# A split becomes an entry of the memory attention's walk, mixed rows are split one step sooner, and GpSimd's first small loads wait for the input's last tile

## The chip, the cores and the metric

One NeuronCore of a Trainium2 chip runs the whole program. The metric is the device time of one execution in microseconds. Three runs of the kernel before gave 2355.81, 2359.80 and 2361.21 us; the median is 2359.8 us.

## The reference, cut to what matters

Two transformer blocks over 512 tokens of width 1024, all in float32. The first block has a mixer (dilated window attention with 8 heads beside a retention with 4), a cross attention to a memory of 256 tokens, and a hierarchical mixture of 32 experts. The second has two layers of attention and a squared-ReLU MLP. The change touches the start of the mixer, its output projection, and the cross attention to the memory:

```python
def memory_cross_attention(h, mem_h, w_mq, w_mkv, q_norm_w, k_norm_w, w_mo):
    q = rms_norm(split_heads(h @ w_mq, MEM_HEADS, MEM_HEAD_DIM), q_norm_w) * (MEM_HEAD_DIM ** -0.5)
    mk, mv = jnp.split(mem_h @ w_mkv, 2, axis=-1)
    k = rms_norm(split_heads(mk, MEM_HEADS, MEM_HEAD_DIM), k_norm_w)
    v = split_heads(mv, MEM_HEADS, MEM_HEAD_DIM)
    s = jnp.einsum('bhsd,bhmd->bhsm', q, k, preferred_element_type=jnp.float32)
    p = jax.nn.softmax(s, axis=-1)
    o = jnp.einsum('bhsm,bhmd->bhsd', p.astype(v.dtype), v)
    return merge_heads(o) @ w_mo

x = x + parallel_mixer(rms_norm(x, norm_mix_w), w_in, ...)
x = x + memory_cross_attention(rms_norm(x, norm_mem_w), rms_norm(mem, norm_memkv_w), ...)
x = x + hierarchical_moe(rms_norm(x, norm_moe_w), ...)
```

There are 4 heads of width 256 here. The 512 queries are 4 token tiles of 128 rows, so there are 16 tiles of 128 queries x 256 keys.

## The kernel before, in words

**Projections.** Each float32 factor is split in two: a high part (rounded to the type fp32r that TensorE takes at full rate) and a low part (the factor less its high part). A product is three matmuls: high x high, high x low, low x high (`three`, L461; `products`, L455). Activations stand transposed in FH and FL. Weights come as units of 1 MB (a quarter-depth panel of 512 x 512 times two) into four raw buffers R; ScalarE writes the high part (`act_cut`, L441, 128 x 2048) and then VectorE the low part (`dve_cut`, L449). A third pair of split buffers serves some units of the memory stage. SyncE sends unit u only once the low part of unit u - 4 is done. A panel of 512 columns needs two units (its half 0 and half 1 of the depth), and `projecting` (L490) walks a list of steps (half, token tile), each of 12 matmuls of 128 x 512.

**Order of work.** Each engine has its own program order, written out by hand; engines wait for each other by semaphores only. Attention is walked (`walk`, L841): a list of entries is passed with a lag for each kind of work. In step s an engine does the scores of entry s, the transposes of the weights of entry s - 2 ("turn"), their products with the values of s - 3 ("apply"), and for an entry whose pair completes a half of a token tile "finish" of s - 3, "even" of s - 4, "store" of s - 5 and "rest" of s - 6. Entries that aren't tiles ("q", "cut", "out") carry other work at the lag that each engine's function gives them.

**The start.** SyncE issues x's tile 0, a small gain, weight unit 0, x's tiles 1 to 3 and then units 1 to 3. GpSimd issues five small loads at once (`pool_mix`, L1034: head gains, decays, a group norm gain, each one row read 128 times); VectorE waits for them at L998, ahead of L999. TensorE transposes each tile of x (L474), VectorE multiplies by the gain (L985), ScalarE writes FH (L948), VectorE FL (L991).

**The output projection of the mixer** (`act_out` L1251, `dve_out` L1327). Units 12 to 15 are w_out. After its steps (1, 0) and (1, 1) TensorE also transposes the normalised memory's tiles 0 and 1 into PSUM banks 6 and 7 (`turn_mem`, L1177); tile 1 takes the two banks that tile 0 had, once tile 0's low parts are written (`mem_lo`, L562). ScalarE cuts unit 14 and then writes the high parts of tile 0; VectorE likewise. Unit 14 goes where unit 12 was, so its cut waits until TensorE has done step (0, 3).

**The memory attention.** `mem_tiles` (L1408) makes 16 tiles, 8 pairs; a pair is one half (two heads) of a token tile. The walk has pairs 0 and 1, the entry "q" (the last transposes of q), pairs 2 to 7 and three entries "out", in which TensorE does the first three steps (0, 0), (1, 0), (0, 1) of the projection w_mo. Before the walk, ScalarE and VectorE cut unit 29 (w_mo, half 1). For each pair: VectorE finds the row minimum of the negated scores (`dve_peak`, L684), ScalarE takes the exponential (L702) and copies one tile of transposed weights (L726), VectorE the other (L738); TensorE applies them (L776) and spreads the reciprocals of the sums (L792), ScalarE copies those (L811), VectorE multiplies (`dve_even_out`, L817), ScalarE writes FH of w_mo's input (`act_mixed`, L823, at "store") and VectorE its FL (`dve_mixed`, L837, at "rest"). w_mo's step (half, i) needs both halves of token tile i.

**After it.** `sp_router` (L1835) sends 2 MB expert loads: load 0 when unit 27 has been used, load 1 into the raw buffers of units 28 and 29 (after unit 29's low part), the others after the last pair has been applied or later. The experts follow, then the second block.

Of the kernel before, what the change touches and what calls it, by code (L numbers as in the profile page):

```python
# [434 lines left out]
def act_cut(k, u):  # L435
    w = k.w
    m = w.units[u][0] * w.units[u][1]
    k.A.wait_ge(*w.landed[u % RAW].at(u))
    if w.prior[u] is not None:
        k.A.wait_ge(*w.freed[w.prior[u]])  # L440
    k.A.e.activation(w.splits[w.split_of[u]][0][:, 0:m], w.rows(u), ACT.Copy).then_inc(*w.hi.tick(u))  # L441


def dve_cut(k, u):
    w = k.w
    m = w.units[u][0] * w.units[u][1]
    wh, wl = w.splits[w.split_of[u]]
    k.V.wait_ge(*w.hi.at(u))
    k.V.e.tensor_tensor(wl[:, 0:m], w.rows(u), wh[:, 0:m].bitcast(F32), ALU.subtract).then_inc(*w.lo.tick(u))  # L449
# [98 lines left out]
def act_features(k, site, i, dst=None):  # L548
    FH, _ = dst or (k.FH, k.FL)
    for half in range(2):  # L550
        k.A.wait_ge(*k.feat_turned.at(site, i, half))
        k.A.e.activation(FH[:, 4 * half:4 * half + 4, 128 * i:128 * i + 128],
                         k.banks[site, i, half][:].rearrange("p (k t) -> p k t", k=4),
                         ACT.Copy).then_inc(*k.feat_hi.tick(site, i, half))
# [241 lines left out]
def evened(k, *key):  # L796
    return k.dve_step.at("evened", *key)
# [56 lines left out]
def pairs(tiles):  # L854
    return list(zip(tiles[0::2], tiles[1::2]))
# [177 lines left out]

def pool_mix(k):  # L1034
    a, sm, ge = k.a, k.m_small, k.G.e
    for n, (dst, src) in enumerate(((sm[:, 0:64], a["attn_q_norm_w"][0]), (sm[:, 64:128], a["attn_k_norm_w"][0]),
                     (sm[:, 128:132], a["ret_decay_f"][0]), (sm[:, 132:136], a["ret_decay_b"][0]),
                     (sm[:, 256:768], a["ret_gn_w"][0]))):
        ge.dma_start(dst, src.partition_broadcast(P)).then_inc(*k.c1_in.tick(n))
    for i in range(NT):  # L1040
        pool_root(k, "mix", i)
    for n in range(8):
        pool_heads(k, "mix", n, 8)
# [207 lines left out]
def act_out(k):  # L1251

    u0 = k.start["w_out"]
    act_cut(k, u0 + 2)
    act_features(k, "mem", 0, k.mem_feats)
    act_features(k, "mem", 1, k.mem_feats)
    act_cut(k, u0 + 3)
    act_cut(k, u0 + 4)
    k.A.wait_ge(*k.mix_lo.at("a1", 3))
    act_cut(k, u0 + 6)  # L1260
    act_cut(k, u0 + 5)
# [64 lines left out]

def dve_out(k):  # L1327
    u0 = k.start["w_out"]
    dve_cut(k, u0 + 2)
    dve_features(k, "mem", 0, k.mem_feats)  # L1330
    dve_add(k, "w_out", 0, 0, None)
    dve_features(k, "mem", 1, k.mem_feats)
    for i in range(1, NT):
        dve_add(k, "w_out", 0, i, None)
    dve_cut(k, u0 + 3)
    dve_cut(k, u0 + 4)
    dve_cut(k, u0 + 6)
    for i in range(NT):
        dve_add(k, "w_out", 1, i, None)
    dve_cut(k, u0 + 5)  # L1340
# [67 lines left out]
def mem_tiles(k):  # L1408
    seq = []
    k.groups["mem"] = [("mem", i, half) for i in range(NT) for half in range(2)]  # L1410
    for i in range(NT):
        for h in range(4):
            n = 4 * i + h

            def values(pt, h=h):
                return [[(k.e_vm[:, c, 256 * h + 128 * half:256 * h + 128 * half + 128], pt[:, 128 * c:128 * c + 128])
                         for c in range(2)] for half in range(2)]
            at = [slice(256 * (h % 2) + 128 * half, 256 * (h % 2) + 128 * half + 128) for half in range(2)]
            q = [k.e_qT[:, 2 * h + c, 128 * i:128 * i + 128] for c in range(2)]
            key = ("mem", i, h // 2)  # L1420
            seq.append(Tile(("mem", n), 256, q[0], k.e_kT[:, 2 * h, :], values, k.zero, (key, evened(k, *key)),
                            slice(0, P), at, spot(k, n // 2, h % 2), full=(h % 2 == 1), more=(q[1], k.e_kT[:, 2 * h + 1, :])))
    return pairs(seq[:4]) + [("q", 3)] + pairs(seq[4:]) + [("out", 0), ("out", 1), ("out", 2)]


def mem_out(k, half, **kw):
# [56 lines left out]
def act_memory(k):  # L1483
    A, u0, u1 = k.A, k.start["w_mkv"], k.start["w_mq"]

    def square(i):
        A.wait_ge(*k.res.at("w_out", 1, i))
        if i >= 2:
            A.wait_ge(*k.feat_turned.at("xm", i - 2, 1))
        act_square(k, "xm", i, k.X[:, i, :], k.x_rows[i % 2])  # L1490
    square(0)
    square(1)
    for p in range(4):
        if p:
            act_features(k, "xm", p - 1)
        if p in (1, 2):
            square(p + 1)
        act_cut(k, u0 + 2 * p + 3)
        for i in range(2):
            if p < 2:  # L1500
                act_heads(k, "memk", 2 * p + i, k.banks["w_mkv", p, i], k.projected.at("w_mkv", p, i))
            else:
                A.wait_ge(*k.projected.at("w_mkv", p, i))
                A.e.activation(k.e_vm[:, i, 512 * p - 1024:512 * p - 512], k.banks["w_mkv", p, i][:],
                               ACT.Copy).then_inc(*k.panel_a.tick("memv", p, i))
            if p in (1, 2):
                act_piece(k, ("memk", p - 1, i), k.e_kT[:, 4 * p - 4:4 * p, :], i)
        act_cut(k, u0 + 2 * p + 4)
    act_features(k, "xm", 3)
    act_cut(k, u1 + 3)  # L1510
    for p in range(2):
        for i in range(NT):
            if (p, i) == (1, 3):
                act_cut(k, u1 + 4)
            act_heads(k, "memq", 4 * p + i, k.banks["w_mq", p, i], k.projected.at("w_mq", p, i))
            if p:
                act_piece(k, ("memq", 0, i), k.e_qT[:, 0:4, :], i)
            if p and i:
                act_piece(k, ("memq", 1, i - 1), k.e_qT[:, 4:8, :], i - 1)
    act_cut(k, u1 + 5)  # L1520
    for what, e in walk(k.seq2):
        if not isinstance(e[0], Tile):
            if e[0] == "q" and what == "turn":
                act_piece(k, ("memq", 1, 3), k.e_qT[:, 4:8, :], 3)
        elif what == "turn":
            act_weights(k, e[0])
        elif what == "score":
            for t in e:
                act_exp(k, t)
        elif what == "finish":  # L1530
            act_over(k, e[1].bank[0])
        elif what == "store":
            key = e[1].bank[0]
            act_mixed(k, key, key[1], 4 * key[2], even_out(k, *key), evened(k, *key))


def dve_memory(k):
    V, ve, u0, u1 = k.V, k.V.e, k.start["w_mkv"], k.start["w_mq"]
    V.wait_ge(*k.c2_in.at(1))
    ve.memset(k.zero, 0.0)  # L1540
    V.settle(ve.tensor_scalar(k.mem_norms[:, 0:256], k.mem_norms[:, 0:256], -1.0 / 16.0, None, ALU.mult))
    V.wait_ge(*k.om_in[0].at("mem"))

    def scale(i):
        dve_scale(k, "xm", i, k.X[:, i, :], k.x_rows[i % 2], k.om[0][:])
    dve_mean(k, "xm", 0)
    dve_mean(k, "xm", 1)
    scale(0)
    scale(1)
    for p in range(4):  # L1550
        if p:
            dve_features(k, "xm", p - 1)
        if p in (1, 2):
            dve_mean(k, "xm", p + 1)
        dve_cut(k, u0 + 2 * p + 3)
        if p in (1, 2):
            scale(p + 1)
        if p < 2:
            dve_heads(k, "memk", 2 * p, 2, 2, k.mem_norms[:, 256:512], lambda i: k.nsp[2 * p + i][:], lambda i: None)
        dve_cut(k, u0 + 2 * p + 4)  # L1560
    dve_features(k, "xm", 3)
    gain = k.mem_norms[:, 0:256]
    dve_cut(k, u1 + 3)
    dve_heads(k, "memq", 0, NT, 2, gain, lambda i: k.nsp[i][:], lambda i: None)
    for i in range(NT):
        if i == 3:
            dve_cut(k, u1 + 4)
        dve_head_means(k, "memq", 4 + i, 2)
        dve_head_rows(k, "memq", 4 + i, 2, gain, k.nsp[i][:] if i < 3 else k.q_last, k.piece_turned.at("memq", 0, i))
    dve_cut(k, u1 + 5)  # L1570
    for what, e in walk(k.seq2):
        if not isinstance(e[0], Tile):
            continue
        if what == "turn":
            dve_weights(k, e)
        elif what == "score":
            for t in e:
                dve_peak(k, t)
        elif what == "finish":
            dve_even_out(k, e[1].bank[0])  # L1580
        elif what == "rest":
            key = e[1].bank[0]
            dve_mixed(k, key, key[1], 4 * key[2], even_out(k, *key))

# [1819 lines left out]
```

## Time and profile before

| | |
|---|---|
| median of 3 runs | 2359.8 us (2355.81 to 2361.21) |
| profiled execution: its own time, its span | 2362.44 us, 2361.1 us |
| TensorE (PE) busy, matmuls | 2236.7 us, 95% |
| VectorE (DVE) busy | 1020.7 us, 43% |
| ScalarE (ACT) busy | 716.6 us, 30% |
| GpSimd (POOL) busy | 103.1 us, 4% |
| mean granted TensorE clock | 0.979 |
| DMA, mean | 157 GB/s |

Times are microseconds from the start of the span. A row of a timeline is: start, length, engine, line, operation, output <- inputs, shape, count, and in brackets the idle time ahead of it and what ended it. PE matmuls overlap each other, so the time from one start to the next says more than a length. A row of the chain of waits is: start, length, what. In a row of windows each engine has its busy time and its count; the last three numbers are the granted clock of TensorE (1.00 is 2.4 GHz, 0.50 is 1.2 GHz), the busy share of the 16 DMA engines and GB/s.

### The profile page before, as it was taken

The numbers are of one execution on the slowest core, as the hardware profiler recorded it, in microseconds if no ns is written. First come the engines' busy times: TensorE is split into PE (matmuls) and PEld (weight loads), VectorE is DVE, ScalarE is ACT, GpSimd is POOL, SyncE is SP. The second block draws the span as 40 slices with busy tenths as digits, with TensorE's granted clock in tenths as the row PEclk, the third lists the DMA queues.
The fourth block names the chain that finished last, engine by engine and source line by source line (L and its number), as shares of the span: only waits on it lengthen the run. The fifth ranks groups of instructions, "written<-read, shape, count | busy, mean of one in ns | idle before, by whom it ended". The sixth has DMA issues, their size and how long they took to land.

```text
span 2361.1 us, 28318 instructions
## 1 busy us (share of the span) xinstructions
PE 2236.7 (95%) x11771; PEld 1647.0 (70%) x11771; DVE 1020.7 (43%) x1858; ACT 716.6 (30%) x1249; POOL 103.1 (4%) x109
## 2 busy tenths in 40 slices
PE   8999899979989889899889999999999999999998
PEld 6866687864433334388656788888878777888887
DVE  5336465342322232443567553234432466433335
ACT  4325354320000000132456233133132462331330
POOL 2101001000000000000000000000000000000001
PEclk9999999989999999999989999999999999999999
DMA  5233343268999999732110232322142201332320
GB/s 194 93 110 108 103 161 109 80 227 365 426 427 427 427 427 427 322 109 87 37 54 2 90 125 90 103 93 93 51 156 89 72 1 59 107 103 90 107 90 36
DMA packets 106740, 370.27 MB, mean 157 GB/s; under 512 B 15168, under 2 KB 20672, under 8 KB 94320
## 3 DMA queue, kind: packets, MB, share of 16 engines
q1 hardware_dynamic: 103584, 361.58, 40.8%
q0 software_dynamic: 3024, 6.83, 0.9%
q8 instruction: 95, 1.56, 0.3%
q14 instruction: 37, 0.30, 0.0%
HBM read 368.32 MB, written 4.19 MB: 158 GB/s over the span
## 4 chain that ended last, share of the span: by engine, by line
PE 82%; DMA 9%; DVE 4%; ACT 2%; issue 1%; POOL 0%; SPq 0%; DVEq 0%; ACTq 0%; POOLq 0%
PE PB L457 56%; PE PB L1934 9%; PE PB L474 5%; PE PB L776 4%; PE PB L467 3%; DMA FL_raw<-in_w_exp_gate 3%; PE PB L668 3%; DMA FH_raw<-in_w_exp_gate 3%; DMA Z<-in_w_exp_gate 1%; DMA W_raw<-in_w_exp_down 1%; PE PB L792 1%; PE PB L673 1%; ACT nsp L702 1%; DMA scratch_h<-Z 1%; DMA X<-in_x 0%
## 5 line engine op out<-in xcount | busy, mean ns | idle before, releaser
L457 PE MATMUL PB<-W,FH 128*128 128x512 f32 (+1 forms) x1792 | 556.0, 392 | 6.1 <-DVE FL L837 5.2
L449 DVE TENSOR_TENSOR W<-R,W 128x2048 fp32r<-128x2048 f32 (+1 forms) x128 | 291.3, 2277 | 606.9 <-ACT W L441 606.9
L441 ACT ACTIVATE W<-R 128x2048 fp32r<-128x2048 f32 (+1 forms) x128 | 243.4, 1902 | 648.8 <-PE PB L457 642.0
L457 PEld LDWEIGHTS PB<-W,FH 128*128 128x128 f32 x1792 | 330.9, 189 | 73.4 <-DVE FL L837 6.3
L457 PE MATMUL PB<-W,hid 128*128 128x512 f32 x1536 | 349.4, 390 | 0.0
L457 PE MATMUL PB<-W,FL 128*128 128x512 f32 (+1 forms) x896 | 348.2, 389 | 0.0
L457 PEld LDWEIGHTS PB<-W,hid 128*128 128x128 f32 x1536 | 288.4, 188 | 59.5
L457 PE MATMUL PB<-FH,W 128*128 128x512 f32 (+1 forms) x1152 | 324.5, 367 | 4.5 <-DVE FL L562 4.5
L457 PEld LDWEIGHTS PB<-FH,W 128*128 128x128 f32 x1152 | 208.7, 189 | 40.5 <-issue 5.0
L457 PE MATMUL PB<-FL,W 128*128 128x512 f32 (+1 forms) x576 | 210.9, 366 | 0.0
L457 PEld LDWEIGHTS PB<-W,FL 128*128 128x128 f32 x896 | 169.2, 189 | 34.7
L1934 PE MATMUL PB<-R,om 128*64 128x512 f32 x320 | 150.7, 627 | 16.7 <-DMA FL_raw<-in_w_exp_gate 9.2
L1934 PE MATMUL PB<-Z,om 128*64 128x512 f32 x304 | 124.7, 611 | 0.8 <-issue 0.8
L457 PEld LDWEIGHTS PB<-FL,W 128*128 128x128 f32 x576 | 108.8, 189 | 17.2
L474 PEld LDWEIGHTS PB<-ident,nsp 128*128 128x128 f32 x674 | 80.2, 148 | 44.6 <-issue 31.3
L474 PE MATMUL PB<-ident,nsp 128*128 128x128 f32 x674 | 103.4, 281 | 7.0 <-ACT nsp L702 3.7
L702 ACT ACTIVATE nsp<-nsp,stat 128x512 f32<-128x512 f32 (+3 forms) x146 | 83.3, 572 | 70.3 <-DVE stat L684 70.0
L2007 ACT ACTIVATE tmp_r<-PB 128x512 fp32r<-128x512 f32 x32 | 17.4, 594 | 262.4 <-PE PB L1934 262.4
L684 DVE CUSTOM_DVE_ANT_0 nsp<-PB,Z 128x512 f32<-128x512 f32 (+3 forms) x146 | 69.1, 510 | 63.5 <-PE PB L668 47.1
L668 PE MATMUL PB<-Z 64*128 64x512 f32 (+4 forms) x416 | 93.5, 512 | 2.7 <-ACT om L2701 1.8
L776 PE MATMUL PB<-ptr,Z 128*64 128x128 f32 (+1 forms) x768 | 79.3, 283 | 14.5 <-ACT ptr L726 8.8
L1934 PEld LDWEIGHTS PB<-R,om 128*64 128x64 f32 x320 | 44.7, 144 | 66.2 <-issue 66.2
(337 smaller groups left out, 2587.4 us busy)
## 6 DMA issues: line engine op xcount, KB each, us to landing
R<-in_mlp_w_up SPq DMA_DIRECT2D x32, 1024.0 KB, 5.3
R<-in_mlp_w_down SPq DMA_DIRECT2D x32, 1024.0 KB, 5.1
Z<-in_w_exp_down SPq DMA_DIRECT2D x14, 2048.0 KB, 29.5
Z<-in_w_exp_up SPq DMA_DIRECT2D x13, 2048.0 KB, 35.2
R<-in_w_exp_gate SPq DMA_DIRECT2D x11, 2048.0 KB, 33.8
W_raw<-in_w_exp_up SPq DMA_DIRECT2D x10, 2048.0 KB, 31.5
R<-in_w_exp_up SPq DMA_DIRECT2D x9, 2048.0 KB, 30.9
R<-in_w_in SPq DMA_DIRECT2D x12, 1024.0 KB, 5.3
```

Source lines behind the costliest of these rows:

```text
L441: k.A.e.activation(w.splits[w.split_of[u]][0][:, 0:m], w.rows(u), ACT.Copy).then_inc(*w.hi.tick(u))
L449: k.V.e.tensor_tensor(wl[:, 0:m], w.rows(u), wh[:, 0:m].bitcast(F32), ALU.subtract).then_inc(*w.lo.tick(u))
L457: ins = te.matmul(bank, l, r, start=(start and n == 0), stop=(stop and n == len(terms) - 1), skip_group_check=True)
L467: ins = te.matmul(bank, l, r, start=(n == 0), stop=(n == len(pairs) - 1))
L474: ins = k.T.e.transpose(bank[0:s.shape[1], 128 * n:128 * n + m], s, k.ident[0:m, 0:m])
L668: ins = k.T.e.matmul(bank[:, 0:t.n], t.q, t.keys, start=True, stop=(t.more is None))
L673: k.T.e.matmul(bank[:, 0:t.n], *t.more, start=False, stop=True).then_inc(*k.scored.tick(*t.key))
L684: V.e.tensor_tensor_reduce(ns[:, 0:t.n], k.banks[("scores",) + t.key][:, 0:t.n], t.tab, 1.0, FAR, ALU.add, ALU.min, peak(k, m)).then_inc(* ...
L702: k.A.e.activation(ns[:, 0:t.n], ns[:, 0:t.n], ACT.Exp, bias=peak(k, m), scale=-1.0, accum_out=t.den).then_inc(*k.exped.tick(*t.key))
L776: ins = T.e.matmul(k.banks["sums", *t.bank[0]][t.rows, at], l, r, start=first, stop=last, skip_group_check=True)
L792: ins = T.e.matmul(bank[rows, 128 * c:128 * c + 128], col, k.ident[:], start=True, stop=True, skip_group_check=True)
L1934: ins = T.e.matmul(bank[64 * side:64 * side + 64, :], lhs[:, 128 * c + 64 * side:128 * c + 64 * side + 64], ws[side][:, c, at], start=(c = ...
```

## The change: what it does, and the diff

- `pool_mix`: GpSimd waits for x's tile 3 before it issues the five small loads.
- `act_out`, `dve_out`: the high and low parts of the memory's tile 0 are written before unit 14 is cut; VectorE also adds w_out's first tile before it.
- `mem_tiles`: the walk gets an entry "cut" between pair 0 and pair 1, so it is one entry longer; ScalarE cuts unit 29 at that entry's "apply" (step 4) and VectorE at its "even" (step 5), no longer both before the walk.
- ScalarE's `act_mixed` moves from "store" to "even", and VectorE's `dve_mixed` from "rest" to "store".

```diff
 def pool_mix(k):
     a, sm, ge = k.a, k.m_small, k.G.e
+    k.G.wait_ge(*k.x_in[3].at())
@@ act_out
     u0 = k.start["w_out"]
+    act_features(k, "mem", 0, k.mem_feats)
     act_cut(k, u0 + 2)
-    act_features(k, "mem", 0, k.mem_feats)
     act_features(k, "mem", 1, k.mem_feats)
@@ dve_out
-    dve_cut(k, u0 + 2)
     dve_features(k, "mem", 0, k.mem_feats)
     dve_add(k, "w_out", 0, 0, None)
+    dve_cut(k, u0 + 2)
     dve_features(k, "mem", 1, k.mem_feats)
@@ mem_tiles
-    return pairs(seq[:4]) + [("q", 3)] + pairs(seq[4:]) + [("out", 0), ("out", 1), ("out", 2)]
+    two = pairs(seq)
+    return two[:1] + [("cut", 0)] + two[1:2] + [("q", 3)] + two[2:] + [("out", 0), ("out", 1), ("out", 2)]
@@ act_memory
-    act_cut(k, u1 + 5)
     for what, e in walk(k.seq2):
         if not isinstance(e[0], Tile):
...
+            elif e[0] == "cut" and what == "apply":
+                act_cut(k, u1 + 5)
...
-        elif what == "store":
+        elif what == "even":
             key = e[1].bank[0]
             act_mixed(k, key, key[1], 4 * key[2], even_out(k, *key), evened(k, *key))
@@ dve_memory
-    dve_cut(k, u1 + 5)
     for what, e in walk(k.seq2):
         if not isinstance(e[0], Tile):
-            continue
-        if what == "turn":
+            if e[0] == "cut" and what == "even":
+                dve_cut(k, u1 + 5)
+        elif what == "turn":
...
-        elif what == "rest":
+        elif what == "store":
             key = e[1].bank[0]
             dve_mixed(k, key, key[1], 4 * key[2], even_out(k, *key))
```

## Rows read from the trace of the kernel before

**Rows 1.** Page, section 4: the chain that ended last, by engine.
```profile
PE 82%; DMA 9%; DVE 4%; ACT 2%; issue 1%; POOL 0%; SPq 0%; DVEq 0%; ACTq 0%; POOLq 0%
```

**Rows 2.** Chain of waits, 0 to 60 us.
```profile
2.15 11.44 DMA X<-in_x
...
13.62 4.80 PE PB L474 x24
18.43 35.65 PE PB L457 x156
```

**Rows 3.** DMA queues, 5 to 10 us: packets, MB, share of 16 engines.
```profile
q1 hardware_dynamic: 464, 1.11, 63.1%
q0 software_dynamic: 102, 0.10, 33.8%
```

**Rows 4.** DMA queues, 10 to 14 us.
```profile
q1 hardware_dynamic: 407, 1.26, 80.1%
q0 software_dynamic: 106, 0.24, 20.2%
```

**Rows 5.** Timeline of all engines at the start.
```profile
11.11 1.91 ACT L441 ACTIVATE W<-R 128x2048 fp32r<-128x2048 f32 x1 [3.35 <-DMA R<-in_w_in]
...
26.58 0.30 PEld L457 LDWEIGHTS PB<-W,FH 128*128 128x128 f32 x2 [0.36 <-DVE FL L991]
...
30.06 0.18 DVE L999 TENSOR_SCALAR Z<-Z 128x64 f32<-128x64 f32 x1
```

**Rows 6.** DMA issues: KB, median us to landing.
```profile
Z<-in_ret_gn_w POOLq DMA_DIRECT2D x1, 256.0 KB, 9.5
```

**Rows 7.** Timelines of ACT, DVE and PE, output projection.
```profile
271.19 1.92 ACT L441 ACTIVATE W<-R 128x2048 fp32r<-128x2048 f32 x1 [6.58 <-PE PB L457]
...
273.14 2.29 DVE L449 TENSOR_TENSOR W<-R,W 128x2048 fp32r<-128x2048 f32 x1 [7.80 <-ACT W L441]
...
276.09 1.36 PE L474 MATMUL PB<-ident,tmp 128*128 128x128 f32 x8 [2.27 <-DVE mem_lo L562]
```

**Rows 8.** Windows: busy us of PE, PEld, DVE, ACT, POOL; clock; DMA.
```profile
164.00:175.00 11.00, 11.00 (x43) 5.73 (x41) 4.68 (x7) 2.03 (x3) 0.00 (x0) 0.53 0.04 15
...
277.00:281.00 4.00, 4.00 (x14) 3.24 (x12) 2.14 (x4) 0.98 (x2) 0.00 (x0) 0.57 0.70 255
...
410.00:414.00 4.00, 3.92 (x13) 3.08 (x14) 1.13 (x5) 1.55 (x7) 0.00 (x0) 0.57 0.85 340
414.00:461.00 47.00, 42.22 (x301) 39.03 (x299) 16.82 (x53) 18.07 (x48) 0.00 (x0) 1.00 0.07 16
461.00:465.00 4.00, 3.94 (x10) 3.14 (x11) 1.16 (x2) 0.00 (x0) 0.00 (x0) 0.57 1.00 190
```

**Rows 9.** Timeline of PE, memory attention.
```profile
409.95 1.16 PE L474 MATMUL PB<-ident,nsp 128*128 128x128 f32 x4 [3.44 <-ACT nsp L702]
...
452.65 0.70 PE L457 MATMUL PB<-W,FH 128*128 128x512 f32 x2 [2.12 <-DVE FL L837]
...
461.06 0.87 PE L457 MATMUL PB<-W,FH 128*128 128x512 f32 x2 [2.72 <-DVE FL L837]
```

**Rows 10.** Chain of waits, memory attention.
```profile
406.62 2.20 DVE W L449
...
422.11 0.87 PE PB L668 x4
...
426.44 1.79 PE PB L776 x16
428.23 0.89 PE PB L792 x8
...
459.75 1.21 DVE FL L837 x2
```

**Rows 11.** Windows around the experts.
```profile
535.00:541.00 6.00, 6.00 (x38) 2.29 (x34) 0.00 (x0) 0.10 (x1) 0.00 (x0) 0.87 0.02 10
...
560.00:960.00 400.00, 369.17 (x1698) 158.54 (x1696) 116.79 (x187) 35.81 (x68) 10.87 (x11) 0.97 1.01 427
```

## Prediction, made before the result was known

> **What bounds the kernel now.** I read the page's chain first: PE holds 82% of it and DMA 9% [rows 1], so the time is TensorE's stream of matmuls plus what it waits for, and the DMA part is the expert stage. Then I read the chain and the engines' timelines in the three places that the diff touches. (a) At the start the chain is a DMA: x's tile 1, issued at 2.15, lands at 13.6; then PE runs without a break [rows 2]. (b) In the output projection PE stands 2.27 us before the transposes of the memory's tile 1, held by `mem_lo`, and then has the low clock [rows 7, 8]. (c) In the memory attention PE stands 3.44 us after its first scores, 2.12 us before w_mo's step (0, 1) and 2.72 us before (0, 2) [rows 9]; two of the three are followed by the low clock [rows 8]. Everywhere between, PE is the chain, so what PE gains there moves all that follows.
>
> Is it kept in the expert stage, where DMA runs at 427 GB/s? That stream starts when PE gives its first buffers back: before it, from 535 to 541, DMA moves 10 GB/s [rows 11]. So it starts as much sooner as PE does, and its length stays.
>
> **Part A, GpSimd's small loads wait (L1038).** They move 0.34 MB, but hold 33.8% of the 16 engines for 5 us and 20.2% for 4 us: 1.69 + 0.81 = 2.5 us of all DMA time ahead of x's landing [rows 3, 4]. SP's own queue moved 1.11 MB in 63.1% of 5 us, which is 352 GB/s had it been alone. Unit 0, landed at 11.11, stands ahead of tile 1 in that queue. From 5 us to that moment the queue moved 1.11 MB and 1.11/4 of 1.26, together 1.46 MB, which alone takes 4.15 us: unit 0 at 9.15, 2.0 sooner; tile 1, after 1.11 + 0.9 x 1.26 = 2.24 MB and 6.4 us, at 11.4, 2.2 sooner. VectorE's chain (cut of unit 0, gains, splits) starts from unit 0 and already ends last at PE's fourth step, where PE waits 0.36 us [rows 5]; so I take the smaller, 2.0 us. The five loads are now issued at about 11.6 to 14.6 (3 us in all, as before) beside units 1 to 3. Unit 1 is needed at 17.7, and by the same rates is in by 15.5, before their packets. VectorE asks for them at L999, 30.06 less 2.0 = 28.1; with the old 9.5 us to landing [rows 6] they are in at 24.1. Cover 4 us. Behind L999 on VectorE stands the cut of unit 2, which starts 1.8 us after it and takes 2.3, so it ended at 34.2; PE wants it after 8 steps of 12 matmuls, 18.43 + 96 x 35.65/156 = 40.4 [rows 2], 6 us later. GpSimd itself has nothing else to do till 27.1. Bounds: nothing, if tile 1 lands when it did (a loss has no place with that cover), to 5 us, if the engines that also served the small loads were the late ones: tile 0, unit 0 and tile 1 are 2.1 MB, 6.0 us at 352 GB/s, so tile 1 could be in by 8.5.
>
> The Trainium skill says in "DMA: Bandwidth & Descriptors" (Queues, rings and completion order) that a DMA engine takes turns between the queues that have work for it, packet by packet. By that rule a small packet takes a turn from x whatever its size; this trace agrees, with 102 packets of 0.10 MB at 33.8% beside 464 of 1.11 MB at 63.1%. It also says in "SBUF — State Buffer" (SBUF: two separate sides) that GpSimd can't write the descriptors of its DMAs while VectorE runs an operation that takes both ports. That speaks against the new place: before, VectorE was idle while the loads were issued, now it cuts unit 0. No row here shows such a stall; by the rule the loads would come late, which is the third rival below.
>
> **Part B, memory tile 0 split before unit 14.** ScalarE has been idle 6.58 us and VectorE 7.80 us when the cut's turn comes [rows 7]; tile 0's transposes are done by 268.1, so two high parts (0.5 us each) and two low parts (0.6 us each) fit before 271.19. The cut of unit 14 stays where it is, ended by PE's step (0, 3). Gone are PE's idle 2.27 us and the low clock behind it: 0.57 over 4 us costs 0.43 x 4 = 1.7 us [rows 8]. Sum 4.0 us. What is late next: unit 14, ready at 275.43, is wanted after two more steps (274.4 + 5.5 = 279.9); unit 15, cut once step (1, 3) has ended, is 10.9 us ahead of need; unit 18, sent by unit 14's low part, has 10 us to spare. Nothing new stands on the path. Bounds: 2.3 us, if the low clock comes all the same, to 4.3.
>
> **Part C, the walk.** Cut 29 took VectorE from 406.62 to 408.82, with pair 0's scores waiting [rows 10]. Without it the transposes of pair 0 start at 407.75, not 409.95. But with the entry there are no scores of pair 2 between "turn" and "apply" of pair 0: apply waits for ScalarE's four exponentials (0.5 us each, from 407.1) and a copy of 0.36, so it starts at 409.5. PE stands 1.3 and then 1.1 us in place of 3.44. From there the steps at full clock are apply 1.79, spread 0.89, scores 1.73, turn 0.44, scores 1.73, turn 0.44, apply 1.79, spread 0.89 = 9.7: pair 4's scores come at 419.2 instead of 422.1. The low clock at 410 to 414 went with the long stall. 2.9 us gained here.
>
> The cut is not free in its new place. VectorE reaches it after `dve_even_out` of pair 1: spread ends 419.2, ScalarE's copy and the product 1.3, so 420.9; cut 2.2 -> 423.1; pair 0's FL 0.6 -> 423.7; then pair 4's minima, 0.45 to the first, exponentials 1.0 and ScalarE's copy 0.36: pair 2 is applied at 425.7, where PE was ready at 423.5. PE stands 2.2 us, and of the 2.9 us 0.7 are left (426.44 before [rows 10]). ScalarE's own cut (1.8 us from 415.9) lies under PE's steps.
>
> From there PE is full up to step (0, 1). It needs pair 3's FL. Before, that came in the walk's step 10, behind `dve_even_out` of pair 6; now it comes behind that of pair 5, and PE gets there one entry later. 2.12 us go. Step (0, 2) needs pair 5's FL, which stands behind `dve_even_out` of pair 7 as before, but no longer behind pair 4's: of the two splits, 1.21 us [rows 10], one goes, 0.6 us; 2.1 of 2.72 us stay. Sum 0.7 + 2.1 + 0.6 = 3.4, with rounding 3.5 us.
>
> The clock: of the stalls before, 2.12 us kept 1.00 and 2.27, 2.72 and 3.44 us were followed by 0.50 [rows 7 to 9]. The new ones are 1.3 + 1.1 close together, 2.2 and 2.1 us, on the edge. I take one low stretch among them, as the one at 461 that is there now. Bounds: 3.5 + 1.7 = 5.2 us with none, 3.5 - 3.4 = 0.1 us with three. Expert load 1 waits for unit 29's low part and moves from 408.85 to about 423; DMA moves under 20 GB/s from 420 to the walk's end, so it is hidden.
>
> **Sum.** 2.0 + 4.0 + 3.5 = 9.5 us. The profiled execution took 2362.44 (span 2361.1), 2.6 above the median of 2359.8; against the median I predict 2350.3 us. Its likeliest case runs from 2346 to 2354.
>
> **Rivals.** (1) The small loads cost x nothing: tile 1 lands by its own queue's length. For it: x and the weights are ten times as many bytes. Against it: unit 0 took 9.4 us to land. Gain 7.5, time 2352.3. 15%. (2) The moved cut gives the walk back: low clock at the new stalls, part C near 0.1. For it: three stalls near 2.2 us. Gain 6.1, time 2353.7; with rival 1, 2355.7. 16%. (3) Slower: the small loads come so late that VectorE stands at L999, with unit 2's cut behind it. It decides only from a landing at 28.1 + 6 (PE's cover) + 9.5 (the rest of the gain) = 43.6 us, 29 us after the last issue, where 9.5 was seen. At 50 us the time would be 2366. 2%. (4) Low stretches elsewhere: the dilated attention has one of 11 us at 0.53 [rows 8], about 5 us lost, and all of it now comes 2 us sooner; a second one gives 2355, two more stretches the old time, three make it slower. 9%, 2% of it slower. The change may also save more than it says: part A at 5 and no low clock in C (5.2) give 2345.6; 8%. The forecast keeps 50%.
>
> **How the numbers follow.** Range 2344 to 2357: from the large case with some spread of the runs (they lay 5.4 us apart) to past rivals 1 and 2 together. This measurement can tell about 0.2%, 4.7 us, from nothing: below 2355.1 is faster. The forecast, the large case and rival 1 lie there, and most of rival 2: 0.84. Same 0.12, slower 0.04.
>
> **What would show it.** Right: x's tile 1 lands near 11.4 and PE's first projection matmul starts near 16.3; no idle before the transposes of the memory's tile 1 and a clock of 1.00 after; in the walk stalls of 1.3, 1.1 and 2.2 us, none before w_mo's (0, 1), 2.1 before (0, 2). Wrong: tile 1 at 13.6; clock 0.50 after three of the walk's stalls; a wait at L999; or a stage far from the three places that changed length by over 2 us.

## The result, and the profile after

The changed kernel takes 2353.22 us (median of 20 runs, 2349.41 to 2357.10), the kernel before 2361.07 us (20 runs, 2355.81 to 2366.76). The ratio is 0.9967, 95% interval 0.9961 to 0.9973, so 7.8 us or 0.33% faster. The forecast was 9.5 us against a median of 2359.8, so 2350.3 us. The profiled execution took 2355.56 us with a span of 2354.2 us, 6.9 less than the span before.

Where the time went is read by laying the two chains of waits side by side: the same piece of the chain, its start after less its start before. After the start that is -1.5 us, after the dilated attention -0.95, after the output projection -5.2, behind the walk -7.9, at the end -6.9. So the start and the dilated attention together gave 0.95 (forecast 2.0), the output projection 4.3 (4.0), the walk 2.7 (3.5), and 1.0 was lost again in stages that the change doesn't touch (by how much such stages differ from profile to profile stands under the table below).

**The start.** The chain of waits of the changed kernel; it answers to [rows 2].

```profile
1.67 7.84 DMA R<-in_w_in
...
11.47 2.29 DVE W L449
...
20.07 2.29 DVE W L449
...
23.66 1.30 DVE FL L991 x2
...
25.00 27.54 PE PB L457 x120
```

The chain no longer begins with x but with weight unit 0. The timeline of PE and the one of GpSimd, same kernel:

```profile
10.85 4.19 PE L474 MATMUL PB<-ident,X 128*128 128x128 f32 x24 [4.47 <-DMA X<-in_x]
14.79 0.71 PE L457 MATMUL PB<-W,FH 128*128 128x512 f32 x2
...
25.00 0.74 PE L457 MATMUL PB<-W,FH 128*128 128x512 f32 x2 [1.77 <-DVE FL L991]
```
```profile
14.02 0.78 POOL L1040 DMA_DIRECT2D Z<-in_attn_q_norm_w  x1 [12.45 <-DMA X<-in_x]
...
16.41 0.57 POOL L1040 DMA_DIRECT2D Z<-in_ret_gn_w  x1
```

x's tile 1 is there at 10.85 (13.62 before) and PE's first projection matmul starts at 14.79, but PE then waits 1.77 us ahead of its fourth step, where it waited 0.36 [rows 5]. That step starts at 25.00, not 26.58: 1.58 us, just what unit 0 is sooner (ScalarE cuts it from 9.53, before from 11.11). The DMA queues from 5 to 10 us answer to [rows 3]: SyncE's queue is alone and moves 1.74 MB, not 1.11.

```profile
q1 hardware_dynamic: 656, 1.74, 96.9%
```

**The output projection.** Chain, and a window of the clock (columns as in [rows 8]):

```profile
272.86 0.87 PE PB L474 x8
273.74 26.32 PE PB L457 x116
```
```profile
277.00:281.00 4.00, 4.00 (x19) 3.33 (x18) 1.10 (x2) 1.70 (x1) 0.00 (x0) 1.00 0.59 226
```

No wait ahead of the transposes of the memory's tile 1, where [rows 7] had 2.27 us, and the full clock where [rows 8] had 0.57.

**The walk.** The rows of PE's timeline with a stall; they answer to [rows 9].

```profile
402.52 0.90 PE L474 MATMUL PB<-ident,nsp 128*128 128x128 f32 x4 [1.24 <-ACT nsp L702]
404.22 2.02 PE L776 MATMUL PB<-ptr,Z 128*128 128x128 f32 x16 [0.80 <-ACT ptr L726]
...
414.13 1.16 PE L792 MATMUL PB<-ident,stat 128*128 128x128 f32 x8 [0.88 <-ACT Z L655]
...
421.28 2.02 PE L776 MATMUL PB<-ptr,Z 128*128 128x128 f32 x16 [1.66 <-DVE stat L684]
...
453.17 0.70 PE L457 MATMUL PB<-W,FH 128*128 128x512 f32 x2 [2.12 <-DVE FL L837]
```

The first, second, fourth and fifth were forecast as 1.3, 1.1, 2.2 and 2.1 us. The third was not: PE waits to spread pair 1's reciprocals. What it waits for stands in the chain just ahead of it:

```profile
410.30 1.80 ACT W L441
412.10 0.52 ACT FH L823
412.62 0.98 ACT nsp L702 x4
413.60 0.49 ACT Z L655
...
414.13 1.17 PE PB L792 x8
```

L655 is ScalarE's copy of q's last transposes out of their PSUM bank. It stands in program order behind the moved cut, a high part that came one step sooner, and the exponentials of pair 3; the spread wants that bank (e9 below shows it by moving the copy). The clock is full behind the first four stalls, and low behind the last:

```profile
453.00:457.00 4.00, 3.83 (x11) 3.07 (x12) 1.27 (x3) 0.13 (x1) 0.00 (x0) 0.62 0.82 144
```

### The profile page after: what moved, and what is told of

The parts are those of the page before. It is cut to its first block, busy times and chain, and to the rows that moved or that the text cites. A ratio compares the mean times of both kernels' runs of the same rounds, so it can differ in the third digit from the quotient of the medians.

```text
span 2354.2 us, 28318 instructions
## 1 busy us (share of the span) xinstructions
PE 2234.6 (95%) x11771; PEld 1644.1 (70%) x11771; DVE 1020.3 (43%) x1858; ACT 716.8 (30%) x1249; POOL 103.1 (4%) x109
## 4 chain that ended last, share of the span: by engine, by line
PE 81%; DMA 9%; DVE 4%; ACT 3%; issue 1%; POOL 0%; SPq 0%; DVEq 0%; ACTq 0%; POOLq 0%
PE PB L457 56%; PE PB L1937 9%; PE PB L474 4%; PE PB L776 4%; PE PB L467 3%; DMA FL_raw<-in_w_exp_gate 3%; DMA FH_raw<-in_w_exp_gate 3%; PE PB L668 2%; DMA Z<-in_w_exp_gate 1%; DMA W_raw<-in_w_exp_down 1%; PE PB L792 1%; PE PB L673 1%; ACT nsp L702 1%; ACT W L441 1%; DMA scratch_h<-Z 1%
```

## The experiments

Twelve kernels ran, in three groups, each beside the kernel before on the same chip (medians of before 2361.0, 2360.52, 2361.33 us). In this table A is the wait of GpSimd, B the order in the output projection, C the walk. The five columns in the middle are offsets of one profiled execution against the profile of before, by the same piece of the chain (its start before: 54.51, behind the first panel; 197.58, in the dilated attention; 396.72, ahead of the walk; 488.27, behind it; 2341.28, the end). The last is the median less the median of before beside it.

| kernel | parts | 54 | 198 | 397 | 488 | end | median |
|---|---|---|---|---|---|---|---|
| changed | A B C | -1.53 | -0.95 | -5.22 | -7.88 | -6.90 | -7.8 |
| e1 | A | -1.39 | -0.28 | -0.28 | -0.17 | -0.24 | -0.4 |
| e2 | B | 1.00 | 2.95 | -0.99 | 0.01 | -4.53 | -3.1 |
| e3 | C | 0.29 | 0.32 | 0.33 | -0.70 | 0.83 | +0.5 |
| e4 | A B C, both cuts sooner | -2.09 | -0.59 | -4.86 | -9.60 | -8.73 | -7.5 |
| e5 | B C | -0.11 | 0.07 | -4.20 | -6.81 | -8.82 | -6.5 |
| e6 | A B | -2.74 | -0.30 | -4.57 | -3.64 | -5.58 | -4.4 |
| e7 | A B C, low parts sooner | -3.50 | -1.27 | -5.51 | -10.39 | -13.26 | -8.1 |
| e8 | e4 + e7 + later cut 1 | -3.05 | -0.71 | -4.98 | -11.96 | -9.27 | -12.9 |
| e9 | A B C, copy first | -1.79 | -1.47 | -5.72 | -10.95 | -9.67 | -11.4 |
| e10 | e8 + e9 | -3.67 | -1.83 | -5.67 | -14.17 | -16.72 | -14.5 |
| e11 | entry of C | 0.18 | 0.47 | -1.08 | 1.34 | -1.14 | +0.2 |
| e12 | mixed rows of C | -1.69 | -1.64 | -3.22 | -4.98 | -9.70 | -4.3 |

From the column 488 to the end no kernel differs from another in what it does, and yet that stretch moved by -4.7 to +2.7 us. The columns 54 and 198 move as well without any edit at the start (from -1.69 in e12 to 2.95 in e2). A single profile therefore tells only what happens at the edited place; the whole is read from the medians, whose intervals in these runs are 0.08 to 0.16% (2 to 4 us) to either side.

**The three parts alone.** e1 is the diff's first hunk by itself, e2 the hunks of `act_out` and `dve_out`, e3 the rest.

```diff
e1  pool_mix
+    k.G.wait_ge(*k.x_in[3].at())
e2  act_out (dve_out likewise, with dve_add)
+    act_features(k, "mem", 0, k.mem_feats)
     act_cut(k, u0 + 2)
-    act_features(k, "mem", 0, k.mem_feats)
e3  mem_tiles, act_memory, dve_memory
     the change as shown; pool_mix, act_out, dve_out as before
```

> The kernel before with part A alone (GpSimd's five small loads wait for x's tile 3). Theory: x's tile 1 lands near 10.9 us (13.6 before), but VectorE's chain from unit 0's landing (9.5, was 11.1) carries only 1.6 us of it to the first projection panel: PE's fourth step starts at 25.0, not 26.6. Time about 1.5 us less than before. Rival 1 (the loads cost x nothing, and the tile came sooner by chance): tile 1 at 13.6, no gain. Rival 2 (all of the tile's 2.8 us is kept): PE's fourth step at 23.8, 2.8 us gained.

> The kernel before with part B alone (the memory's tile 0 split before unit 14 is cut). Theory: the idle 2.3 us of PE and the low clock after it both go, 4.2 us; the clock is 1.00 from 270 to 290. Rival (a low stretch comes whatever the stall): only the idle goes, 2.3 us, and the clock is at 0.5 somewhere between 270 and 300.

> The kernel before with part C alone (entry for the cut, mixed rows one step sooner). Theory: 2.7 us of the walk, up to w_mo's step (0, 2), and the low clock after that step stays or goes by chance (1.7 us): 2.7 to 4.4 us in all. Rival (parts help each other, the walk gains only because it is earlier): under 1 us.

Measured: e1 2360.63 us, ratio 0.9996 (0.9987 to 1.0005); e2 2357.91, 0.9989 (0.9980 to 0.9999); e3 2361.46, 0.9997 (0.9987 to 1.0007). e1's median is 0.4 us below the kernel before where its theory had 1.5, and it is known to 2.1. At their places A and B do what they do in the changed kernel: 1.4 us at the start for A, of which 0.28 are left at 198, and 3.9 us for B (2.95 to -0.99), with the full clock as its theory said. But B's profile gives 1.0 us back in the walk (-0.99 to 0.01). Part C missed its theory of 2.7 us or more: its walk gains 1.03 us (0.33 to -0.70), and its median is the rival's. It has the stalls of the changed kernel to within 0.01 us, but the low clock comes after the second of them, beside the one behind (0, 2) that both kernels have. Window of the clock in e3, and the row of PE's timeline ahead of it:

```profile
410.00:414.00 4.00, 4.00 (x23) 4.00 (x23) 0.00 (x0) 0.00 (x0) 0.00 (x0) 0.57 0.01 2
```
```profile
409.77 3.04 PE L776 MATMUL PB<-ptr,Z 128*128 128x128 f32 x16 [0.79 <-ACT ptr L726]
```

The changed kernel at the same place, one step after the same stalls:

```profile
404.00:408.00 4.00, 3.78 (x29) 3.71 (x30) 0.20 (x1) 0.72 (x2) 0.00 (x0) 1.00 0.01 2
```

**Two parts each.** e5 is the changed kernel without the wait in `pool_mix`, e6 the kernel before with the wait and the new order of the output projection.

```diff
e5  pool_mix, against the changed kernel
-    k.G.wait_ge(*k.x_in[3].at())
e6  mem_tiles, act_memory, dve_memory as in the kernel before
```

> The changed kernel without part A: GpSimd's small loads are issued at once, as before; tile 0's order and the walk are the changed ones. Alone, part A moved the median by 0.4 us, part B by 3.1 and part C by -0.5 (slower), together 3.0, while all three together gave 7.8. Theory 1, the parts simply add in the trace (1.6, 4.3 and 2.7 us at their own places) and what the medians of single parts lack is one stretch of the low clock more or less in stages that no part touches: this kernel gains 4.3 + 2.7 = 7.0 at the two places against the kernel before, and its median lies at 2354 to 2356 with up to 1.7 us per stretch on top. Theory 2, the parts need each other: without A's shift of 1.5 us the low clock comes back in the memory's attention as in the run of part C alone (a stretch at 411 to 414), and the walk is again only 0.7 ahead: 2358 to 2360.

> The kernel before with parts A and B, the walk unchanged. Theory 1 (the parts add at their own places): 1.6 + 4.3 = 5.9 less the 0.6 that A loses again in the dilated attention, so 5.3 us less than the kernel before, 2355.7, by one or two stretches of the low clock more or less (1.7 us each). Theory 2 (the parts need each other): the medians of A and B alone add, 0.4 + 3.1 = 3.5, 2357.5, and C's place in the sum of 7.8 is 4.3 though alone it gave nothing.

Measured: e5 2354.04 us, ratio 0.9973 (0.9962 to 0.9983); e6 2356.13, 0.9979 (0.9969 to 0.9989). So A is worth 0.4 us alone and 1.3 on top of B or of B and C; B 3.1 alone, 4.0 on A, 7.0 on C; C -0.5 alone and 3.4 on B or on A and B. For e5 theory 1 holds and theory 2 doesn't: without A's shift the walk is as in the changed kernel (-2.61 against -2.66). e6 lies between its two forecasts, 2355.7 and 2357.5, and can't tell them apart.

Alone the parts add to 3.0 us, together they give 7.8. The four intervals (2.1, 2.2, 2.4 and 1.4 us to either side), combined as if independent, make 4.1 us, and the gap is 4.8: chance alone is unlikely, but not excluded.

The profiles show where such a gap can come from. With B, C is worth 3.6 us in the walk (e5 gains 2.61 where e2 loses 1.00; the changed kernel gains 2.66 where e6 loses 0.93), alone 1.03. Both sides of it are the clock. First, the low clock after the walk's first stalls came in both profiles of the entry without B (e3, e11) and in none of the seven with B (the changed kernel, e4, e5, e7 to e10). Second, without the entry every profile has a low stretch behind the stall of 3.44 us, but it is longer in e2, e6 and e12 than in the kernel before and e1: the same work up to w_mo's (0, 2) takes 0.9 us more, after the stalls are taken off. Behind the end of the stall, at 409.95, the kernel before has 0.57 for 4 us and the full clock from 414 [rows 8]. In e12 the stall ends at 406.72, and this is the window:

```profile
406.00:413.00 7.00, 6.28 (x22) 5.29 (x23) 3.01 (x14) 3.79 (x14) 0.00 (x0) 0.51 0.81 301
```

e12 has no B, so the longer stretch doesn't need B. How an order 130 us earlier would set the clock in the walk no run shows, and each side rests on two or three profiles.

**The two halves of C.** e11 has only the entry, e12 only the sooner mixed rows.

```diff
e11  against e3
-        elif what == "even":       (act_memory)
+        elif what == "store":
-        elif what == "store":      (dve_memory)
+        elif what == "rest":
e12  against the kernel before
-        elif what == "store":      (act_memory)
+        elif what == "even":
-        elif what == "rest":       (dve_memory)
+        elif what == "store":
```

> The kernel before, of part C only the entry: cut 29 in the walk behind pair 0, and the mixed rows split at their old steps. Prediction's working: the entry is worth 2.9 - 2.2 = 0.7 us at pair 2's apply; the 2.12 us before w_mo's step (0, 1) are there again, since pair 3's low part stands behind pair 6's even rows, and about 0.6 less before (0, 2) than with both. So -0.7 to 0 at pair 2 and at most 1 us gained at (0, 2). Rival: without high and low parts of pair 0 ahead of pair 3's exponentials and pair 4's minima, both engines reach these 0.5 to 0.6 us sooner, and the entry alone is worth 1.9 us or more at pair 2. In the median up to 1.7 us per stretch of the low clock either way: 2358 to 2362.

> The kernel before, of part C only the mixed rows one step sooner; cut 29 ahead of the walk. Prediction's working: 2.1 us before w_mo's step (0, 1) go and 0.6 us before (0, 2), the start of the walk stays (3.44 us stall, low clock 410 to 414): 2.7 us gained at (0, 2), 2358. Rival: the sooner splits stand ahead of the next pair's exponentials and minima and cost 0.5 us at some apply steps, and the stall before (0, 2), up to 2.7, brings its low stretch all the same: 1.5 to 2 us gained, 2359 to 2360.

Measured: e11 2361.52 us, ratio 1.0001 (0.9990 to 1.0012); e12 2356.99, 0.9983 (0.9975 to 0.9992). Stalls of PE's timeline in e11, and then in e12:

```profile
406.67 0.90 PE L474 MATMUL PB<-ident,nsp 128*128 128x128 f32 x4 [1.24 <-ACT nsp L702]
408.37 3.61 PE L776 MATMUL PB<-ptr,Z 128*128 128x128 f32 x16 [0.80 <-ACT ptr L726]
...
419.35 1.16 PE L792 MATMUL PB<-ident,stat 128*128 128x128 f32 x8 [0.36 <-ACT Z L655]
425.90 2.02 PE L776 MATMUL PB<-ptr,Z 128*128 128x128 f32 x16 [1.06 <-ACT ptr L726]
...
452.41 0.98 PE L457 MATMUL PB<-W,FH 128*128 128x512 f32 x2 [2.12 <-DVE FL L837]
462.38 0.74 PE L457 MATMUL PB<-W,FH 128*128 128x512 f32 x2 [2.72 <-DVE FL L837]
```
```profile
406.72 1.15 PE L474 MATMUL PB<-ident,nsp 128*128 128x128 f32 x4 [3.44 <-ACT nsp L702]
...
456.06 0.70 PE L457 MATMUL PB<-W,FH 128*128 128x512 f32 x2 [2.12 <-DVE FL L837]
```

The entry turns one stall of 3.44 us into four of 1.24 + 0.80 + 0.36 + 1.06 = 3.46: it gains nothing. The two stalls before w_mo's steps (0, 1) and (0, 2) are untouched by it in length, but the first of them, which kept the full clock in the kernel before, is followed by 0.58 here (452 to 456). So e11's walk loses 2.42 us (-1.08 to 1.34), where at most 1 us gained was expected. The mixed rows take away 2.12 and 0.60 us there, as forecast, though e12's walk is only 1.78 us ahead at (0, 2) and not 2.7, by the longer low stretch behind its 3.44 us. With the entry they add 0.52 and 0.60 us to the entry's third and fourth stall (0.88 and 1.66 with both), since their splits then stand ahead of exponentials and minima. e11's rival was right in that size, and wrong that the entry would be worth 1.9 us. In the medians the mixed rows alone give 4.3 us, the entry alone -0.2, and the two as part C (e3) -0.5, so the mixed rows may be the whole of C's gain. A, B and the mixed rows without the entry were not run; what the entry is worth beside B stays open.

**Where the cut goes.** e4 has ScalarE's cut 29 at the entry's "turn" and VectorE's at its "apply", one step sooner each. In the changed kernel ScalarE stands idle 3.05 us at the first place, and VectorE 4.46 us at the second.

```diff
-            elif e[0] == "cut" and what == "apply":   (act_memory)
+            elif e[0] == "cut" and what == "turn":
-            if e[0] == "cut" and what == "even":      (dve_memory)
+            if e[0] == "cut" and what == "apply":
```

> The changed kernel with unit 29's cut in the engines' idle gaps: ScalarE at the entry's turn (step 3, between the copy of pair 0's weights and the copy of its spread), VectorE at its apply (step 4, ahead of dve_even_out of pair 1, which waits 4.5 us). Theory (the place of the cut costs the walk two stalls, 0.9 us at pair 1's spread behind ScalarE's cut, 1.7 us at pair 2's apply behind VectorE's): both go, w_mo's (0, 2) starts 2.5 us sooner, time about 2.5 us below the changed kernel. Rival (the stalls come from the empty entry itself, which takes a pair's scores out from between turn and apply): both stay, time as the changed kernel's.

Measured: 2353.5 us, ratio 0.9966 (0.9955 to 0.9977). PE's stalls in e4:

```profile
402.88 0.90 PE L474 MATMUL PB<-ident,nsp 128*128 128x128 f32 x4 [1.24 <-ACT nsp L702]
404.58 2.02 PE L776 MATMUL PB<-ptr,Z 128*128 128x128 f32 x16 [0.80 <-ACT ptr L726]
414.32 1.16 PE L792 MATMUL PB<-ident,stat 128*128 128x128 f32 x8 [0.71 <-ACT Z L655]
451.47 1.19 PE L457 MATMUL PB<-W,FH 128*128 128x512 f32 x2 [2.12 <-DVE FL L837]
```

The stall at pair 2's apply is gone, which shows that VectorE's cut at "even" made it. Of the stall at pair 1's spread, which the theory took away too, 0.71 us are left: the minima of pair 3 now stand behind VectorE's cut, and ScalarE waits 1.52 us for them ahead of the exponentials and the copy. The walk is worth 4.74 us (-4.86 to -9.60), 2.08 more than in the changed kernel; the median, for which the theory had 2.5 us less, doesn't show it (7.5 against 7.8, known to 2.6 and 1.4 us).

**The low parts one step sooner, and the copy first.** e7 moves VectorE's `dve_mixed` to "even"; e9 puts ScalarE's copy of q's last piece ahead of pair 3's exponentials.

```diff
e7  dve_memory
-        elif what == "store":
+        elif what == "even":
e9  act_memory
-            if e[0] == "q" and what == "turn":
-                act_piece(k, ("memq", 1, 3), k.e_qT[:, 4:8, :], 3)
...
         elif what == "score":
+            if e is k.seq2[5]:
+                act_piece(k, ("memq", 1, 3), k.e_qT[:, 4:8, :], 3)
```

> The changed kernel with VectorE's low parts of the mixed rows one step sooner again, at the step at which VectorE writes the even rows. Theory: the stall of 2.12 us before w_mo's step (0, 2) is pair 5's low part standing behind the even rows of pair 7; with the low part sooner the stall goes, and with it the low clock behind it (453.9 to 457.3 at 0.62, about 1.3 us): gain up to 3.4 us against the changed kernel, 2350. Rival: VectorE's low part now waits for ScalarE's high part of the same pair, which is written in the same step, so it holds VectorE up ahead of the next pair's minima, and stalls of 0.5 to 1 us come at the apply steps: 0 to 2 us gained or lost.

> The changed kernel; ScalarE copies the last piece of q out of its bank ahead of the exponentials of pair 3, not behind them. Theory: the stall of 0.88 us before pair 1's spread is PE waiting for that bank, and the copy ends at 413.1 instead of 414.1 (ScalarE's cut ends at 412.0, the high part takes 0.5, the copy 0.57), so the spread starts at 413.2; what VectorE does behind it moves along, the stall of 1.66 us at pair 2's apply stays: 0.9 us gained in the walk, against the changed kernel's offset of -2.67 at w_mo's step (0, 2) so -3.5, and the median within its scatter (2352 to 2354). Rival: the spread waits for the exponentials and not for the copy (the profile names only the last of several waits): then the stall stays at 0.9, or the exponentials, 0.5 later, make it 1.4.

Measured: e7 2352.38 us, ratio 0.9969 (0.9958 to 0.9980); e9 2349.9, 0.9952 (0.9936 to 0.9968). In e7 the stall before (0, 2) falls from 2.12 to 0.84 us and is released by ScalarE's copy of the reciprocals, no longer by a low part; but the wait for the bank grows from 0.88 to 2.09 us, since VectorE's low part now waits for ScalarE's high part ahead of pair 3's minima. Both theories of e7 were half right: PE stands 6.02 us in all where it stood 6.70 (the five stalls above), 0.7 less and not 2.1; the rest of what its walk gained (4.88 against 2.66 us) is the low clock behind (0, 2), and in the median 0.3 us are to be seen. PE's timeline of e7:

```profile
415.09 1.16 PE L792 MATMUL PB<-ident,stat 128*128 128x128 f32 x8 [2.09 <-ACT Z L655]
...
421.64 2.02 PE L776 MATMUL PB<-ptr,Z 128*128 128x128 f32 x16 [1.06 <-ACT ptr L726]
...
452.24 0.70 PE L457 MATMUL PB<-W,FH 128*128 128x512 f32 x2 [0.84 <-ACT Z L811]
```

e9 settles what the third stall is: with the copy at 412.05 the spread follows the apply without a wait, and the stall behind it stays as it was. Timelines of ScalarE and of PE in e9:

```profile
411.53 0.62 ACT L823 ACTIVATE FH<-Z 128x512 fp32r<-128x512 f32 x1
412.05 0.58 ACT L655 ACTIVATE Z<-PB 128x512 f32<-128x512 f32 x1
412.53 0.50 ACT L702 ACTIVATE nsp<-nsp,stat 128x256 f32<-128x256 f32 x1
```
```profile
411.73 1.06 PE L776 MATMUL PB<-Z 128*128 128x128 f32 x8
412.68 1.16 PE L792 MATMUL PB<-ident,stat 128*128 128x128 f32 x8
...
419.83 2.02 PE L776 MATMUL PB<-ptr,Z 128*128 128x128 f32 x16 [1.66 <-DVE stat L684]
```

Up to w_mo's step (0, 2) e9 gains 3.62 us (-5.72 to 451.72 - 461.06 = -9.34), the changed kernel 2.67: 0.95 more, forecast 0.9. Behind (0, 2) its clock stayed full as well, 1.6 us more, which the same stall of 2.12 us doesn't explain. The median, 2349.9, lies below the 2352 to 2354 that were expected; its interval is 3.8 us to either side.

**Together.** e8 joins e4, e7 and a third edit: units' cut 1 on both engines after x's tile 3. e10 adds e9's edit.

```diff
e8  act_mix and dve_mix, beside the edits of e4 and e7
-        if i in (0, 2):
+        if i in (0, 3):
```

> The changed kernel with four edits: both engines' cuts of unit 29 one step sooner (a gap of each engine; alone it gave 2.06 us more at the walk's end), VectorE's low parts at the step of the even rows, and units' cut 1 after x's tile 3 instead of after tile 2 on both engines. Theory: walk gains 2.06 + up to 3.4, and the stall of 1.77 us at PE's step (0, 3), unit 0, goes, since cut 1 (2.2 us on VectorE) no longer stands ahead of tile 3's gains: together 5 to 7 us, 2346 to 2348. Rival: cut 1 is then the late one, at PE's first step on unit 1, and low stretches in the dilated and the even attention move: 2350 to 2354, no better than the changed kernel.

> The kernel of four edits (both cuts in gaps, VectorE's low parts with the even rows, units' cut 1 after x's tile 3) plus ScalarE's copy of q's last piece ahead of pair 3's exponentials. There the stall before pair 1's spread was 1.31 us and ScalarE idle from 411.1 to 413.2. Theory: the copy finds its place in that idle time and 1.3 us go: walk offset of -8.3 instead of -6.97 us, median 2346.4 against 2347.7. Rival: VectorE, whose cut then ends at 412.2 with pair 3's minima behind it, is late at the next apply and takes 0.5 to 1.3 back: 2347 to 2348.

Measured: e8 2347.66 us, ratio 0.9942 (0.9928 to 0.9956); e10 2346.79, 0.9941 (0.9925 to 0.9956). Both beat the changed kernel, whose interval begins at 0.9961. The walk is worth 6.98 us in e8 and 8.50 in e10 (columns 397 and 488); the copy takes away the stall of 1.31 us that e8 has ahead of pair 1's spread. Neither profile has a low stretch in the walk, so part of both sums is the clock. At the start, PE's projection in e8 runs without a stall once x is there, from this chain:

```profile
2.14 8.85 DMA X<-in_x
...
11.04 4.57 PE PB L474 x24
15.61 35.41 PE PB L457 x156
```

but of the 3.05 us gained there 0.71 are left in the dilated attention, where the kernels with A and without this edit keep 0.28 to 1.47; e10, which has it too, keeps 1.83. Two profiles can't show that this edit brings anything.

## Why the prediction came out as it did

**Part A, 2.0 forecast, 0.95 in the profile, 0.4 to 1.3 in the medians.** The mechanism was right: small packets gone, SyncE's queue moves 1.74 MB in 5 us, 348 GB/s (352 forecast), VectorE's chain from unit 0 ends last at PE's fourth step, the loads land by 16.98 + 6.8 = 23.8 (24.1), and no wait at L999, which runs at 28.49 (28.1). Unit 0 was in at 9.51, not 9.15, and that is the whole of 1.58 against 2.0. The step that failed is that PE's gain would move all that follows. At 156.9 the chain waits for the tables of the dilated attention, a DMA: it took 3.93 us before and 4.31 in the changed kernel, and by the next piece on ScalarE (L726, 162.12 for 163.12) the offset is -1.0. Chain of waits of the changed kernel, then of e7:

```profile
156.24 4.31 DMA Z<-in_c_ntab
```
```profile
153.94 4.91 DMA Z<-in_c_ntab
```

Over all profiles this load took 3.9 to 4.9 us, and not longer the sooner it was due (e10, 3.67 us sooner at the start, had 4.12). Of 1.4 to 3.7 us gained at the start in the eight profiles with A, 0.3 to 1.8 are left at 198 us. Where the start gained most (e6, e7, e8, e10), the larger part went behind the tables, 1.4 to 1.6 us: the low clock there begins sooner (0.56 from 160 to 165 in e7, 0.95 in the kernel before) and ends about where it did (at 175). That is rival 4's stretch, grown longer and not doubled; in the changed kernel it cost what it did before.

How much of the start is A? x's tile 1 was there at 10.67 to 14.11 in the six profiles without A and at 8.66 to 11.04 in the eight with it. e12, without A, is 1.69 us ahead at the start, more than e1, so one profile doesn't prove it. On the mean the kernels with A are 2.4 us ahead of those without at column 54, and 1.3 us at column 198, and 1.3 is what the medians say for A on top of B.

Rival 1, 2352.3 us, is 0.9 us from the measured time, but not for its reason: x did come sooner.

The Trainium skill says in "DMA: Bandwidth & Descriptors" (Queues, rings and completion order) that an engine takes turns between its queues packet by packet; with the small packets gone their 33.8% went to x and the weights, which agrees with it. It warns in "SBUF — State Buffer" (SBUF: two separate sides) that GpSimd can't write descriptors while VectorE runs an operation that takes both ports. The five issues took 2.96 us in the new place (14.02 to 16.98), as long as before (1.88 to 4.84) with VectorE idle: no such stall shows here. It isn't a test of the warning, though. The cut of unit 0 was over at 13.76, and all that VectorE ran beside the issues were TENSOR_TENSOR operations of 128 x 512 (L985, L991); whether these take both ports no run shows. Rival 3 didn't come.

**Part B, 4.0 forecast, 4.27 measured** (columns 198 and 397), 4.24 to 4.27 in seven of the nine kernels that have it, 3.8 and 3.9 in the others. The idle time of 2.27 us went in each. The second term, 1.7 us of low clock, is less firm than the trace of before made it: e11 and e12 keep the stall of 2.27 us and have the full clock behind it. PE's timeline and a window of e11:

```profile
276.58 1.25 PE L474 MATMUL PB<-ident,tmp 128*128 128x128 f32 x8 [2.27 <-DVE mem_lo L562]
```
```profile
277.00:281.00 4.00, 4.00 (x22) 3.22 (x20) 2.88 (x6) 1.20 (x2) 0.00 (x0) 1.00 0.80 266
```

There the kernel without B is already 1.5 us better (0.47 to -1.08). So B is worth 2.7 us at its place whatever the clock does, and 1.5 more when the low clock would have come; that the forecast of 4.0 was met so closely is in part the luck of the profile that it was read from.

**Part C, 3.5 forecast, 2.67 measured** up to (0, 2). Of its terms, 2.12 us before (0, 1) and 0.6 before (0, 2) are right. Failed is "0.7 us are left" at pair 2's apply: there the changed kernel is 0.06 us behind its offset at the walk's start. Up to pair 0's apply the working holds: 409.5 less the 5.22 of A and B is 404.28, and it starts at 404.22. Then the wait for the bank was missed, 0.88 us: the working followed who hands data to whom, and not who holds a PSUM bank. Pair 4's scores come at 415.13, where 419.2 less 5.22 is 413.98. Of these 1.15 us the wait is 0.88, and the slower groups behind stalls are 0.17 (the spread takes 1.16 us after a stall and 1.06 without, the apply 2.02 and 1.95); 0.1 is left, about the tail of the group ahead of the stall. The stall at pair 2's apply gives a little of it back, 1.66 where 2.2 were forecast, and the apply starts at 421.28, 0.80 behind 425.7 less 5.22. That is the whole difference of 3.5 and 2.67. The clock came as forecast, one low stretch where there had been two; the forecast had called this the edge, and with the same stalls e3 had two, and with all but one of them e9 had none, so here too the hit is partly luck.

Read by e11 and e12, the forecast's 0.7 us for the entry is zero: it only divides the stall of 3.44 us. What it can win is the low clock behind that stall, and in e3 and e11 the clock fell all the same.

**Rival 2**, that the moved cut gives the walk back, names 2353.7, and the median was 2353.22. It isn't what happened in the changed kernel, where the clock stayed full at the new stalls up to (0, 2). e3 comes nearer to it: low clock after the second new stall, and 1.03 us of the walk gained.

**The whole.** The three places gave 7.9 us in the profile and 7.8 in the medians; the stages behind lost 1.0 in this profile, and gained or lost up to 4.7 in others. The forecast of 2350.3 was 2.9 us low: 1.05 in A, 0.8 in C, and 1.3 because the median of before moved from 2359.8 to 2361.07 with more runs (which made the time higher at the same gain), less 0.3 in B. The measured time lies nearer to the two rivals than to the forecast.

## What to carry to other kernels

When work is moved inside a software-pipelined walk, follow three things at its new place, on each engine: the data, the program order, and the buffers, PSUM banks above all; a short copy that frees a bank belongs ahead of long work, not behind it. Put a long piece where its engine is idle in the trace (4 us here), not one step later. Try the halves of an edit apart beside the rest of the change before keeping both: here the new entry alone gained nothing. A gain at the start of a program has to pass every later wait and every later stretch of the low clock, and a gain booked for the clock is a chance, not a sum.

## What the runs showed of the hardware that was not expected

- The same stall is followed by either clock. PE's 2.12 us ahead of w_mo's (0, 2), in nearly the same code: 0.62 in the changed kernel, 1.00 in e9. The 2.27 us of the output projection: 0.57 in the kernel before and in e3, 1.00 in e11 and e12. The 2.12 us ahead of (0, 1): 1.00 in the kernel before, e1, e2 and e6, 0.58 in e11. Even 1.24 and 0.80 us with 0.90 us of transposes between them were followed by 1.2 GHz in e3 and e11. The window of e9 behind that stall:

```profile
452.00:460.00 8.00, 8.00 (x37) 6.61 (x36) 0.82 (x2) 0.00 (x0) 0.00 (x0) 1.00 0.84 220
```

- A low stretch costs about 1.7 us (0.43 of 4 us) as a rule, but behind the same stall of 3.44 us it cost 0.9 us more in e2, e6 and e12 than in the kernel before and e1. One profile has more or fewer of them than the next in stages that are the same; with single runs up to some 5 us around the median, the walk's 2.1 us in e4 couldn't be seen in seven runs.
- Four loads of 32 KB and less landed 5.1 to 5.5 us after their issue beside a full queue of weights (6.8 to 7.9 at the start of the program), and the one of 256 KB after 6.8, where [rows 6] had 9.5.
